# Sixteen places for the expert weights in a hybrid transformer layer, filled during the routing, and the general path moved ahead of the combination

## What is computed

```python
def _hier_moe(h, w_rg, b_rg, w_re, b_re, w_g, w_u, w_d):
    ...
    ids = gsel * EXPERTS_PER_GROUP + pi
    combine = jnp.sum(jax.nn.one_hot(ids, N_EXPERTS, dtype=jnp.float32) * wts[..., None], axis=1)
    out = jnp.zeros((b * s, d), jnp.float32)
    for e in range(N_EXPERTS):
        he = jax.nn.silu(t @ w_g[e]) * (t @ w_u[e])
        out = out + combine[:, e:e + 1] * (he @ w_d[e])
    return out.reshape(b, s, d).astype(h.dtype)
...
    h = h + gate1 * (merged @ w_o)
    hn2 = _rmsnorm(h, norm2_g) * (1.0 + scale2) + shift2
    h = h + gate2 * _hier_moe(hn2, ...)
...
    return _rmsnorm(h, final_g)
```

## Time and profile before

| what | value |
|---|---|
| median of the runs | 3028.64 us |
| time of the profiled execution | 3029.07 us |
| its span in the profile | 3027.3 us |
| PE busy in the span | 2747.6 us (91%) |
| DVE, ACT, POOL busy | 50%, 32%, 11% |
| mean DMA rate over the span | 116 GB/s |

### The profile page before, as it was taken

The page is one execution under the profiler, slowest core; times in us unless marked ns, Lnnn a source line. Parts: engine busy times, 40 slices in busy tenths (PEclk is TensorE's granted clock), DMA queues, the critical chain, the costliest instruction groups (busy, mean ns, idle before and its releaser), DMA issues. The chain is left out here.

```text
span 3027.3 us, 35013 instructions
## 1 busy us (share of the span) xinstructions
PE 2747.6 (91%) x14285; PEld 2130.2 (70%) x14285; DVE 1523.4 (50%) x2159; ACT 981.7 (32%) x1360; POOL 320.9 (11%) x187
## 2 busy tenths in 40 slices
PE   6899999999998999999997999999987798979784
PEld 4777687888786777788885887887765565865442
DVE  4662255544538424545555644655735686454103
ACT  3244433222322444322222322333511387311011
POOL 0000004432200000124440000001000000001100
PEclk8999999999999999999998989999988798979996
DMA  4211124444312112433341322343333200249992
GB/s 127 70 60 48 46 87 136 139 127 139 91 56 70 50 48 65 131 113 124 125 139 56 98 74 84 102 88 109 112 119 106 84 1 3 80 172 419 417 416 108
DMA packets 274745, 351.28 MB, mean 116 GB/s; under 512 B 55060, under 2 KB 251924, under 8 KB 261908
## 3 DMA queue, kind: packets, MB, share of 16 engines
q1 hardware_dynamic: 266036, 327.97, 32.3%
q0 software_dynamic: 8448, 20.98, 1.9%
q10 hardware_dynamic: 96, 0.02, 0.0%
HBM read 332.13 MB, written 25.17 MB: 118 GB/s over the span
## 5 line engine op out<-in xcount | busy, mean ns | idle before, releaser
L196 PE MATMUL ps<-h_hi,w_hi 128*128 128x512 f32 x1760 | 719.0, 409 | 59.6 <-DVE room L815 20.6
L197 PE MATMUL ps<-h_lo,w_hi 128*128 128x512 f32 x1760 | 706.0, 401 | 0.0
L198 PE MATMUL ps<-h_hi,w_lo 128*128 128x512 f32 x1760 | 704.8, 400 | 0.0
L173 ACT ACTIVATE w_hi<-w_raw 128x2048 fp32r<-128x2048 f32 (+1 forms) x170 | 322.3, 1896 | 895.2 <-PE ps L198 886.9
L178 DVE TENSOR_TENSOR w_lo<-w_raw,w_hi 128x2048 fp32r<-128x2048 f32 (+1 forms) x170 | 428.2, 2519 | 256.6 <-ACT w_hi L173 256.5
L196 PEld LDWEIGHTS ps<-h_hi,w_hi 128*128 128x128 f32 x1760 | 338.1, 192 | 153.1 <-issue 71.5
L198 PEld LDWEIGHTS ps<-h_hi,w_lo 128*128 128x128 f32 x1760 | 337.2, 192 | 82.2
L197 PEld LDWEIGHTS ps<-h_lo,w_hi 128*128 128x128 f32 x1760 | 337.8, 192 | 79.0 <-issue 1.9
L196 PE MATMUL ps<-merged_hi,w_hi 128*128 128x512 f32 x640 | 253.4, 396 | 0.0
L198 PE MATMUL ps<-merged_hi,w_lo 128*128 128x512 f32 x640 | 253.3, 396 | 0.0
L197 PE MATMUL ps<-merged_lo,w_hi 128*128 128x512 f32 x640 | 253.3, 396 | 0.0
(11 more groups left out here) (451 smaller groups left out, 3883.0 us busy)
## 6 DMA issues: line engine op xcount, KB each, us to landing
w_raw<-in_w_in SPq DMA_DIRECT2D x284, 256.0 KB, 3.6
w_raw<-in_w_up SPq DMA_DIRECT2D x128, 256.0 KB, 3.5
w_raw<-in_w_down SPq DMA_DIRECT2D x128, 256.0 KB, 3.5
room<-in_w_ada SPq DMA_DIRECT2D x96, 256.0 KB, 6.0
expert_second<-in_w_exp_up SPq DMA_DIRECT2D x17, 1024.0 KB, 14.9
expert_second<-in_w_exp_down SPq DMA_DIRECT2D x16, 1024.0 KB, 15.7
expert_second<-in_w_exp_gate SPq DMA_DIRECT2D x15, 1024.0 KB, 15.5
w_raw<-in_w_exp_gate SPq DMA_DIRECT2D x10, 1024.0 KB, 15.3
```

Source lines behind the costliest of these rows:

```text
L173: act.activation(self.hi[:, q, :, 0:cols], raw[:, q, :, 0:cols], ACT.Copy).then_inc(self.hi_ready, 1)
L196: pe.matmul(out, w[0], x[0], start=start, stop=False)
L197: pe.matmul(out, w[0], x[1], start=False, stop=False)
L198: return pe.matmul(out, w[1], x[0], start=False, stop=stop)
```

## The change

1. The weights of the experts now come in 48 steps of two pieces (both experts of a pair), and there are 8 places for steps, so 16 pieces instead of 8. Place 0 is a tensor of its own (`expert_first`), place 1 is `w_raw`, places 2 and 3 lie over `w_hi` and `w_lo` (`expert_over_w`), places 4 and 5 over `merged_two_hi` and `merged_two_lo` (`expert_over_m`), places 6 and 7 over `h_hi` and `h_lo` (`expert_over_h`). For that the split tensors move to the right end of SBUF. The results of `moe` get 4 buffers (`results`, over `merged`) instead of 2.
2. SP issues all eight first steps in `nsa_end`: step 0 at its start, 1 to 5 as the tensors under them are done with, then the stores of the token rows, and then steps 6 and 7.
3. In `nsa_end` POOL scales and shifts three of the eight half rows (t = 2 first half, t = 3 both halves), each in two instructions, where DVE did each in one.
4. The lists of rows are found with one product at rounded float32 with two equal columns (`ones_r`) instead of a float32 product with one column. In `moe`, `turn(0)` and `gate(0)` go ahead of `find(2)`.
5. The branch to the general path stands ahead of `combine`, not behind it, and `combine` has tensors of its own. The general path is not entered.

```diff
-PIECES = [(kind, i, e) for kind, i in [(0, 0), (1, 0)] + [...] for e in range(2)]
-BUFFERS, EARLY = 8, 7
+STEPS = [(0, 0), (1, 0)] + [step for i in range(1, NP_ + 1) for step in ((0, i), (1, i), (2, i - 1)) if step[1] < NP_]
+PLACES = 8
...
     def piece(self, kind, i, e):
-        b = PIECE_AT[kind, i, e] % BUFFERS
...
+        place = STEP_AT[kind, i] % PLACES
+        if place == 0:
+            return self.w_first[:, e, :]
+        if place == 1:
+            return self.W.raw[:, e].rearrange("p k n -> p (k n)")
+        if place < 4:
+            return self.w_over_w[:, 2 * e + place - 2, :]
+        return self.w_over_m[:, 2 * (place - 4) + e, :] if place < 6 else self.w_over_h[:, 2 * (place - 6) + e, :]
...
+                self.issue_step(sp, 0)
                 self.issue2(sp, P_NSAO, P_MOE)
-                for n in range(EARLY):
-                    if n < 2:
-                        sp.wait_ge(W.lo_ready, 2 * (WO + 1) + n + 1)
-                    if n == 3:
-                        W.done(sp, *wo[3])
-                    self.issue_piece(sp, n)
+                sp.wait_ge(W.lo_ready, 2 * (WO + 1) + 2)
+                self.issue_step(sp, 1)
+                W.done(sp, *wo[2])
+                self.issue_step(sp, 2)
+                W.done(sp, *wo[3])
+                for n in range(3, 6):
+                    self.issue_step(sp, n)
                 for t in range(TB):
-                    sp.wait_ge(rows_ready, t + 1)
+                    if t < 3:
+                        sp.wait_ge(rows_ready, t + 1)
+                    if t >= 2:
+                        sp.wait_ge(rows_made, 2 * t - 3)
                     sp.dma_start(d["rows"][toks(t), :], self.h_tok[:, t, :]).then_inc(rows_stored, 16)
+                sp.wait_ge(turned, KC)
+                for n in range(6, PLACES):
+                    self.issue_step(sp, n)
...
                 dve.wait_ge(kept, KC)
-                for t in range(TB):
-                    if t >= 2:
-                        rows(t, 0)
-                    rows(t, 1)
+                rows(0, 1)
+                rows(1, 1)
+                rows(2, 1)
...
             def _(pool):
                 pool.sem_clear(clear)
+                def rows(t, half, count):
+                    part = slice(half * S, half * S + S)
+                    pool.tensor_scalar(self.h_tok[:, t, part], self.h_tok[:, t, part], self.rs_tok[:, t:t + 1], None, ALU.mult).then_inc(rows_scaled, 1)
+                    pool.wait_ge(rows_scaled, count)
+                    pool.tensor_tensor(self.h_tok[:, t, part], self.h_tok[:, t, part], shift.rearrange("p c s -> p (c s)")[:, part], ALU.add).then_inc(rows_made, 1)
+                pool.wait_ge(rs_ready, 1)
+                pool.wait_ge(kept, KC // 2)
+                rows(2, 0, 1)
+                rows(3, 0, 2)
+                pool.wait_ge(kept, KC)
+                rows(3, 1, 3)
                 pool.wait_ge(rows_stored, 16 * TB)
...
-                for n in range(EARLY, len(PIECES)):
-                    if n >= BUFFERS:
-                        kind, i, _ = PIECES[n - BUFFERS]
-                        sp.wait_ge((gate_done, up_done, down_done)[kind], i + 1)
-                    self.issue_piece(sp, n)
+                for n in range(PLACES, len(STEPS)):
+                    kind, i = STEPS[n - PLACES]
+                    sp.wait_ge((gate_done, up_done, down_done)[kind], i + 1)
+                    self.issue_step(sp, n)
...
-                find(2)
                 turn(0)
                 gate(0)
-                find(3)
+                find(2)
                 turn(1)
                 up(0)
+                find(3)
...
-            mm = pe.matmul(out[:, i:i + 1], ids[:, t, :], self.c("ones")[:, 0:1], start=t == 0, stop=t == TB - 1)
+            mm = pe.matmul(out[:, 2 * i:2 * i + 2], ids[:, t, :], self.ones_r[:], start=t == 0, stop=t == TB - 1)
...
                 self.nsa_end()
                 self.moe()
-                self.combine()
             pool = self.stages.last
-            with nc.If(nc.values_load(self.passes[0:1, 0:1], min_val=0, max_val=1) > 0):
+            with nc.If(nc.values_load(self.passes[0:1, 0:1], min_val=0, max_val=1) > 0), ExitStack() as rest:
+                W.split_places(rest, "rest_w")
+                self.h = self.halves(rest, "rest_h")
...
             self.stages.last = pool
+            self.combine()
         self.finish()
```

More of the change, by code:

```diff
@@ L145, with __init__ @@
 class Weights:
-    def __init__(self, nc, ctx):
+    def __init__(self, nc, ctx, until_experts):
         self.nc = nc
-        sb = lambda n, dt: ctx.enter_context(nc.sbuf_tensor(n, [P, 2, KC, COL], dt))
-        self.raw, self.hi, self.lo = sb("w_raw", F32), sb("w_hi", F32R), sb("w_lo", F32R)
+        self.raw = ctx.enter_context(nc.sbuf_tensor("w_raw", [P, 2, KC, COL], F32))
+        self.split_places(until_experts, "w")
         sem = lambda n: ctx.enter_context(nc.semaphore(n))
@@ L159, in __init__, with split_places @@
         self.elsewhere = 0
+    def split_places(self, ctx, name):
+        self.hi, self.lo = (ctx.enter_context(self.nc.sbuf_tensor(f"{name}_{n}", [P, 2, KC, COL], F32R, side="right")) for n in ("hi", "lo"))
     def issue(self, sp, m, q, quarters, first=False):
@@ L260, in __init__ @@
         self.x = sb("x", [P, KC, S])
-        self.h = (sb("h_hi", [P, KC, S], F32R), sb("h_lo", [P, KC, S], F32R))
         self.ps = ctx.enter_context(nc.psum_tensor("ps", [P, 8, 512], F32))
@@ L264, in __init__, with halves @@
         self.par = sb("par", [P, 96])
+    def halves(self, ctx, name):
+        return tuple(ctx.enter_context(self.nc.sbuf_tensor(f"{name}_{n}", [P, KC, S], F32R, side="right")) for n in ("hi", "lo"))
     def sb(self, name, shape, dt=F32):
@@ L2915, in hidden @@
                     pe.wait_ge(xg_ready, i + 1)
-                    for e in range(2):
-                        pe.wait_ge(*self.piece_landed(kind, i, e))
+                    self.landed(pe, kind, i)
                     w = [self.piece(kind, i, e) for e in range(2)]
@@ L2942, in down @@
                 def down(i):
-                    for e in range(2):
-                        pe.wait_ge(*self.piece_landed(2, i, e))
+                    self.landed(pe, 2, i)
                     pe.wait_ge(u_ready, i + 1)
@@ L3116, in combine @@
             landed = [[sem(f"landed{i}{t}") for t in range(TB)] for i in range(2)]
-            first, second = self.h_tok, self.w_second[:, 0:2, :].rearrange("p a n -> p (a n)").rearrange("p (t d) -> p t d", t=TB)
+            first, second = (st.enter_context(nc.sbuf_tensor(f"results_{n}", [P, TB, D], F32)) for n in ("first", "second"))
             block = st.enter_context(nc.Block())
@@ L3191, in _ @@
                         dve.wait_ge(low, k - 1)
-                    link(dve.tensor_tensor(part, h_hi[:, k, :].bitcast(F32), h_lo[:, k, :].bitcast(F32), ALU.add))
-                    link(dve.tensor_tensor(part, part, rs[:], ALU.mult))
+                    link(dve.scalar_tensor_tensor(part, self.x[:, k, :], self.p2("g2", k, 1), rs[:], ALU.mult, ALU.mult))
                     dve.tensor_scalar(part, part, self.p2("ada", 3 * KC + k, 1), None, ALU.add).then_inc(normed, 1)
@@ L3422, in second @@
                         self.ssd()
-                    self.merged = sbuf(until_moe, "merged2", [P, KC, S], side="right")
+                    until_sum = until_moe.enter_context(ExitStack())
+                    self.merged = sbuf(until_sum, "merged2", [P, KC, S], side="right")
                     self.ssm_out()
```

64 lines of the change are left out of this document (35 added, 29 removed).

## The result

The changed kernel takes **2985.37 us** (median of 4 runs, 2984.24 to 2986.77) against 3028.56 us of the kernel before, timed beside it: a ratio of 0.9859, 95% interval 0.9842 to 0.9876. Its profiled execution took 2985.15 us for a span of 2983.4 us, 43.9 less than the span of 3027.3 before.

A forecast was written before the change was run, and what follows sets the result against it. The expert stage was taken as bound by bytes, PE waiting for the weight stream. From the median 3028.64 us, -20.2 - 1.8 - 2.5 = -24.5 us gave 3004.1 us, range 2999.5 to 3010.5.

The forecast's parts named there:

- the edits costed at nothing: Early step 0, rounded list products, four result buffers, and new addresses in the earlier 2560 us: 0 us.
- The places: Rival: new SBUF addresses slow the split products, 29 us per percent, 3062 us at 2%; chance 0.02.
- Term A: Experts' weight stream in `moe`: 8 pieces fewer, since 16 are in SBUF when it starts; -20.2 us.
- a lower rate in the unheld phase: While PE runs unheld on the stock, the stream might move 402 instead of 416 GB/s, costing 3.7 us; taken as 0.
- Term B: When the weight stream starts, over the end of `nsa_end` and front of `moe`: -1.8 us, bounds -5.8 to +6.2.
- Contention and three half rows less on DVE: In `nsa_end`, DVE saves 2.0 us of half rows but loses 2.5 us beside POOL's instructions.
- The gather: First gather, issued at about 2695.1 behind four new pieces, takes 7 us and lands at 2702; bounds 2.6 and 11.6.
- The front of `moe`: `turn(0)` starts at 2702, not 2703.77, since pair 2's list products no longer precede it; the rest as before.
- Term C: Branch moved ahead of `combine`: -3.5 us at the end, 1.0 us for SP ahead of it; -2.5 us in all.
- ACT's row: Trace of ACT skipping about 60 rows without a stall, taken as the model for SP's branch, costing 1.0 us.
- The signs that I had named: New profile: stream starts between 2708 and 2716, 84 MB, rate 416; gaps or changed stages before 2560 would mean wrong.

The follow-up runs named there:

- both_right: The kernel before with only `w_hi`, `w_lo`, `h_hi` and `h_lo` moved to the right end of SBUF; 3003.01 us.
- aligned: `last_two_later` with unused bytes ahead of `merged_0`, `merged_1` and `yn`, so their distance to the split weights is 0 modulo 1,024; 2960.83 us.
- rows_on_dve: `last_two_later` with all six half rows of the second part on DVE again and no vector instruction on POOL; 2979.2 us.
- last_two_later: The changed kernel with SP issuing steps 6 and 7 at the start of `moe`, not behind the stores in `nsa_end`; 2978.62 us.
- branch_behind: `last_two_later` with the general path behind the combination again, which takes its result buffers as in the kernel before; 2979.6 us.

## Why the prediction was wrong

**The sign was right and the size wrong, by the missing term.** The step that failed stands among the edits costed at nothing: "The earlier 2560 us have the same instructions, with other addresses." That was worth 24.5 us up to `nsa_end`, and 1.5 more in it (`both_right` 134.5 us, before 136.0). The places were named as a rival, but as one that makes the kernel slower, with 0.02: I gave the effect the wrong direction and should have given its size on either side.

Nothing in the trace of the kernel before bore this out. The rival's sign, 409 ns for `h_hi` against 396 for `merged_hi`, was none: both groups were slow (233.3 ns from start to start), and with both fast, in `aligned`, 403 stands against 389. The text was right to put that difference down to something other than the place. The rival's price of 29 us for each percent was wrong. The products overlap: the six groups sum to 2890 us of durations, more than the 2747.6 us in which PE is busy at all. 7,200 products at 233 ns are 1680 us, so a percent is 17 us. The 5,280 with `h` came 2.5% closer, which is 31 us, and about 25 of it reached the time.

The Trainium skill, TensorE: Matmul & The Clock Gate, section Step-by-step: what each phase is for, says that loading the next weights takes no read bandwidth from the running product, since the two operands have read ports of their own. By that rule the distance between them would make no difference; the runs show 6 to 7 ns of 233 from start to start, by the distance alone, so the measurement decides, at least for these products.

**Term A, -20.2: right.** From the start of the stream to the last down product that it holds (2911.63 us; 2953.92 before) it is 221.5 us against 240.4, so -18.9. The range had kept 3.7 us for a lower rate in the unheld phase, and that is not where the missing 1.3 went. The first 90 us run at 409 GB/s and the rest of the window at 415, and the kernel before shows 410 and 415 for the same parts. The low rate of the earlier trace rows belongs to the first microseconds, as the forecast had taken it. The end differs: the changed kernel moves 374 GB/s from 2902 to 2907 and 315 or less behind that, where the one before still moves 421 in the 5 us up to 2950.

**Term B, -1.8: +1.1, and by other causes.** From the start of `nsa_end` to that of the stream it is 150.6 us against 149.5. The places took 1.5 off, so the term itself is +2.6. The range of -5.8 to +6.2 held it, but of its parts only the contention was right.
- *Contention and three half rows less on DVE:* forecast -2.0 + 2.5. By `rows_on_dve` the two cancel to 0.4 us; the growth of DVE's chain beside POOL was 2.3. The Trainium skill, GPSIMD Engine Reference, section Key points, says that GpSimd contends with DVE instructions that run in a 2-port perf mode or have two SBUF inputs. By that rule, the trace agrees: 1.44 us instead of 0.50 for four products of two tiles. The `TENSOR_SCALAR` of 1.07 us instead of 0.17 has one SBUF input, and no run shows in which mode it ran.
- *The gather:* forecast to land at 2702 with the stage starting where it did at 2700. The step that failed is "the stage ends about where it did: POOL drains from 2696.1 for 3.74 us": a transfer ahead of the gather was priced in the gather's landing, but not in the drain that waits for that landing. It cost 6.9 us at the barrier.
- *The front of `moe`:* it took 9.2 us from the barrier to the first free place, before 13.5: 4.3 us less, where the forecast had 1.8. The forecast let the turn wait for the gather until 2702. But the drain had waited for the gather already, so it had landed when the barrier opened, in the changed kernel as in `last_two_later` with its short drain, where the turn starts at 2673.37 behind a barrier at 2673.2 and the front takes 9.2 us too. So the whole 3.7 us of list products that stood ahead of the turn were gained, and 0.7 in the gate products (granted clock 0.58 in this part, before 0.53).

**Term C, -2.5: -1.5 in the changed kernel, -2.6 in `branch_behind`'s pair.** Both parts were mis-sized by similar amounts, and of opposite sign. At the end not 3.5 but 4.5 to 5.1 us were gained; in the changed kernel 3.8 of the 4.5 lie between DVE's last update and PE's first square product (0.96 us, before 4.75), and 0.7 in PE's 16 products (9.74 us, before 10.47). At the front not 1.0 but 2.5 to 3.0 us came to the stage, of which the first load's delay is 1.1 to 1.3. I had sided with ACT's row against the page that spoke for a stall, Runtime: NRT & Kernel Launch, section Instruction fetch mechanics of the Trainium skill. By that rule, the trace agrees on PE (2.83 us of issue in `branch_behind`), and SP's late first load fits it as well, though no run shows that either was a fetch.

**The sum of the spans:** places -24.5 and -1.5; drain +6.9; front -4.3; contention, within the rounding; stream -18.9; from the last down product to `moe`'s barrier -0.1; combination and behind -1.5. That is -43.9, as measured.

**The signs that I had named** came out so: the stream has 84 MB on the hardware queue by forecast, 82.68 by the trace up to 2909, no gap, the rate 413; its start at 2690 was outside the 2708 to 2716, and the stages before 2560 changed their length, which the text had called the sign of a wrong prediction.

## What to carry to other kernels

When a change moves allocations, compare the distance between the operands of the costly products before and after, not only the instructions; here a multiple of 256 bytes between the split weights and the other operand was worth 6 to 7 ns on products that start 233 ns apart, and a tensor of 32 bytes could take it away. Judge such products by the distance of their starts, since durations that overlap count twice when they are summed. When transfers are put ahead of a stage's end, ask which queue must drain there, since POOL's drain waited here for a gather that flowed behind them. And work that goes to POOL beside a busy DVE should be priced with what DVE loses: here it lost about as much as it was spared.

## What the runs showed that I had not expected

- Products of 128x512 (float32, split) at the same code and count start 227 or 233 ns apart by the distance of their operands modulo 256 bytes.
- A POOL drain of 3.6 to 4.3 us became 10.6 us when four 1 MB pieces were issued on SP's queue in the 5 us ahead of the gathers.
- A `TENSOR_SCALAR` of 16 elements in a partition took 1.07 us on DVE beside a POOL sum, until that sum ended, and 0.17 without it.
